# Reordered work at the seams of a two-block transformer kernel: squares with eight buffers, weight halves and loads in another order

## The reference

```python
# block 1
xn = rms_norm(h, norm_mix_g);  proj = xn @ w_in        # q, k, v of stick-breaking attention, q, k, v, g of retention
h = h + (g_sb * (y_sb @ w_sb_out) + g_ret * (y_ret @ w_ret_out)) @ w_out
hn = rms_norm(h, norm_ffn_g)
# 4 groups of 4 experts: best group, its two best experts, each (silu(x @ w_gate) * (x @ w_up)) @ w_down
h = h + hierarchical_moe(hn, ...);  h = rms_norm(h, norm_final_g)
# block 2
proj = rmsnorm(x, norm_mix_g) @ w_in                   # sparse attention with a top-128 index, and q_b, k_b, v_b
x = x + heads @ w_out
x = x + cross_attention(rmsnorm(x, norm_cross_g), rmsnorm(mem, norm_mem_g)) @ w_o_cross     # 256 memory tokens
x = x + square(relu(rmsnorm(x, norm_mlp_g) @ w_up)) @ w_down
return rmsnorm(x, norm_final_g)
```

## Time and profile before

| | |
|---|---|
| median of three runs | 1749.81 us |
| profiled execution | 1747.31 us |
| its span | 1745.5 us |
| PE busy | 1640.7 us (94%) |
| DVE busy | 949.8 us (54%) |
| ACT busy | 747.6 us (43%) |
| POOL busy | 648.5 us (37%) |
| clock of PE granted over the span | 0.978 |

### The profile page before, as it was taken

One profiled execution on the slowest core, in us unless ns is written; L12 is line 12 of the kernel. 1 busy time (PEld: TensorE's weight loads), 2 busy tenths in 40 slices (PEclk: granted clock), 3 DMA queues, 4 the chain that ended last, 5 costly groups with the idle time before them and its releaser, 6 DMA issues. The chain is left out here.

```text
span 1745.5 us, 21103 instructions
## 1 busy us (share of the span) xinstructions
PE 1640.7 (94%) x7992; PEld 1331.5 (76%) x7992; DVE 949.8 (54%) x1123; ACT 747.6 (43%) x895; POOL 648.5 (37%) x261
## 2 busy tenths in 40 slices
PE   7999999899999899999947989899999999999996
PEld 7898788668787888888846857766786788888884
DVE  6514310377164589999857779694443454141413
ACT  6344413234334588888834142475324332222221
POOL 1332154313434133442234726563331434343441
PEclk9999999999999999999978989999999999999998
DMA  6421034212223699999942313400321222222221
GB/s 236 144 73 49 25 110 141 102 35 95 97 101 125 269 422 421 392 387 394 382 166 86 125 49 109 136 1 1 140 77 33 87 97 97 96 96 97 97 96 48
DMA packets 46740, 250.31 MB, mean 143 GB/s; under 512 B 9456, under 2 KB 10224, under 8 KB 19920
## 3 DMA queue, kind: packets, MB, share of 16 engines
q1 hardware_dynamic: 40912, 238.89, 36.9%
q0 software_dynamic: 5184, 8.40, 1.3%
q10 hardware_dynamic: 576, 2.10, 0.3%
HBM read 239.20 MB, written 14.68 MB: 145 GB/s over the span
## 5 line engine op out<-in xcount | busy, mean ns | idle before, releaser
L148 POOL TENSOR_TENSOR w_lo<-raw,w_hi 128x2048 fp32r<-128x2048 f32 x95 | 437.6, 4607 | 704.5 <-ACT w_hi L142 704.4
L227 PE MATMUL psum<-x_hi,w_hi 128*128 128x512 f32 x840 | 329.6, 392 | 10.8 <-POOL w_lo L148 5.9
L228 PE MATMUL psum<-x_lo,w_hi 128*128 128x512 f32 x840 | 327.0, 389 | 0.0
L229 PE MATMUL psum<-x_hi,w_lo 128*128 128x512 f32 x840 | 326.9, 389 | 0.0
L142 ACT ACTIVATE w_hi<-raw 128x2048 fp32r<-128x2048 f32 x100 | 191.0, 1910 | 317.1 <-PE psum L229 315.6
L1296 DVE TENSOR_TENSOR moe_lo<-moe_w,moe_hi 128x2048 fp32r<-128x2048 f32 x99 | 225.6, 2291 | 31.7 <-ACT moe_hi L1286 30.7
L1286 ACT ACTIVATE moe_hi<-moe_w 128x2048 fp32r<-128x2048 f32 x99 | 189.3, 1915 | 27.0 <-PE psum L229 21.4
L227 PEld LDWEIGHTS psum<-x_hi,w_hi 128*128 128x128 f32 x840 | 157.7, 188 | 47.8 <-DVE x_lo L402 5.7
L228 PEld LDWEIGHTS psum<-x_lo,w_hi 128*128 128x128 f32 x840 | 157.7, 188 | 33.1 <-issue 0.7
L229 PEld LDWEIGHTS psum<-x_hi,w_lo 128*128 128x128 f32 x840 | 157.7, 188 | 33.0
L429 DVE TENSOR_TENSOR res<-res,psum 128x512 f32<-128x512 f32 x56 | 38.4, 687 | 217.6 <-PE psum L229 217.6
(11 more groups left out here) (369 smaller groups left out, 2999.8 us busy)
## 6 DMA issues: line engine op xcount, KB each, us to landing
raw<-in_w_dense SPq DMA_DIRECT2D x101, 1024.0 KB, 4.8
moe_w<-in_w_moe_ahead SPq DMA_DIRECT2D x54, 1024.0 KB, 14.2
moe_w<-in_w_moe SPq DMA_DIRECT2D x48, 1024.0 KB, 14.6
yrow<-expert_rows SPq DMA_DIRECT2D x8, 512.0 KB, 10.0
res<-in_x SPq DMA_DIRECT2D x4, 512.0 KB, 11.2
decay<-in_decay SPq DMA_DIRECT2D x8, 256.0 KB, 3.8
hn_rows<-hn_tok ACTq DMA_DIRECT2D x4, 512.0 KB, 2.7
out<-res SPq DMA_DIRECT2D x4, 512.0 KB, 2.6
```

What stands on the lines that cost most here:

```text
L148: pool.tensor_tensor(w_lo[c % RING][:, :], raw[c % RING][:, :], w_hi[c % RING][:, :].bitcast(F32), ALU.subtract).then_inc(lo_ready, 1)
L227: pe.matmul(out, lh, rh, start=first, stop=False)
L228: pe.matmul(out, lh, rl, start=False, stop=False)
L229: return pe.matmul(out, ll, rh, start=False, stop=last)
```

## The change

Six things are edited. (1) `Norm` takes further square buffers (`more_sq`); norm1 has eight, so its squares wait for no add. (2) At start-up SP issues chunk 2 ahead of the third group of x, ACT and DVE take three squares, gained copies and low halves before chunk 2's halves, and PE runs 30 warm-up products in place of 26. (3) In `residual_act` the eighth block's gained copy stands ahead of the next chunk's high half. (4) The memory's high half moves from 96 to 88 KB, off the third expert chunk's high buffer; that chunk is split within k_mem; SP loads expert chunks 0 to 2 at once and 3 to 5 after both gathers have landed; PE reads the number of rounds within k_mem. (5) The low half of q_idx's first chunk goes from POOL to DVE. (6) In q_rope, q_b and k_b POOL makes the low half ahead of the rotation's adds.

```diff
     def dense_pool(pool, name, after=None, halves_first=False):
...
-                if after:
+                if after and not halves_first:
                     after(pool, i, b)
                 split_lo(pool, c0 + 2 + b, i)
+                if after and halves_first:
+                    after(pool, i, b)
...
         def square(self, act, kt):
-            if kt >= 2:
-                act.wait_ge(n_added, (KT - 1) * self.u + kt - 1)
-            act.activation(self.sq[kt % 2][:, :], self.x[:, kt, :], ACT.Square).then_inc(n_squared, 1)
+            if kt >= len(self.sq):
+                act.wait_ge(n_added, (KT - 1) * self.u + max(1, kt - len(self.sq)))
+            act.activation(self.sq[kt % len(self.sq)][:, :], self.x[:, kt, :], ACT.Square).then_inc(n_squared, 1)
...
         for t in range(KT):
-            if t % 2 == 1:
+            if t % 2 == 1 and t < KT - 1:
                 split_hi(act, c0 + 2 + t // 2, t0 + t + 1)
             act.wait_ge(bank_free, t0 + t + 5)
             if gained:
                 gained(t)
+            if t == KT - 1:
+                split_hi(act, c0 + 2 + t // 2, t0 + t + 1)
             norm.square(act, t)
...
-    norm1 = Norm("norm1", res, "mix", 152, hi=x_hi, lo=x_lo, bank=4)
+    norm1 = Norm("norm1", res, "mix", 152, hi=x_hi, lo=x_lo, bank=4, more_sq=(144, 146, 148, 150, 164, 166))
...
         for g in range(4):
+            if g == 2:
+                load_chunk(sp, 2)
             sp.dma_start(res[:, 2 * g:2 * g + 2, :], d["x"][:, 2 * g:2 * g + 2, :]).then_inc(x_landed[g], 16)
-        load_chunk(sp, 2)
...
-        split_lo(dve, 2)
         norm1.add_square(dve, 2)
         x_low(2)
+        split_lo(dve, 2)
...
         square(0)
+        square(1)
         v_mem_out(0)
-        square(1)
         x_high(0)
         x_high(1)
+        square(2)
+        x_high(2)
         v_mem_out(1)
         split_hi(act, 2, 2)
-        square(2)
-        x_high(2)
...
-        for _ in range(26):
+        for _ in range(30):
...
-    m_high = at("mem_hi", 96, [P, KT, MEM], FR)
+    m_high = at("mem_hi", 88, [P, KT, MEM], FR)
...
-            if c == 2:
-                sp.wait_ge(hn_stored, 32)
+            if c == 3:
+                sp.wait_ge(xg_landed[0], 16)
+                sp.wait_ge(xg_landed[1], 16)
             sp.dma_start(ring[c][:, :], d["w_moe_ahead"][PAIRS - 1, c]).then_inc(moe_landed[c // 2], 16)
...
-                             5: lambda: moe_rows_t(pe, 0, 0)})
+                             5: lambda: [moe_rows_t(pe, 0, 0), rounds_read.append(rounds_of(pe))]})
...
             moe_split_chunk(act, 0, 1)
+            moe_split_chunk(act, 0, 2)
...
-        for b in range(2):
-            moe_low_chunk(dve, 0, b)
-            moe_rows_low(dve, 0, b)
+        moe_low_chunk(dve, 0, 0)
+        moe_rows_low(dve, 0, 0)
+        moe_low_chunk(dve, 0, 1)
+        moe_low_chunk(dve, 0, 2)
+        moe_rows_low(dve, 0, 1)
...
     def project_gpsimd(pool):
-        split_lo(pool, KEYS_C + 2)
...
+        pool.wait_ge(lo_ready, KEYS_C + 3)
         split_lo(pool, KEYS_C + 3)
...
-            dense_pool(pool, name, after=lambda e, i, b: rot2.pool(e, name, b))
+            dense_pool(pool, name, after=lambda e, i, b: rot2.pool(e, name, b), halves_first=True)
...
         dve.tensor_tensor(kc_t[0][:, :], psum[:, (KEYS_T + 1) % 4, :], cos_k[:, :], ALU.mult).then_inc(bank_free, 1)
+        dve.wait_ge(lo_ready, KEYS_C + 2)
+        split_lo(dve, KEYS_C + 2)
```

More of the change, by code:

```diff
@@ L176, in dense_sync, with dense_pool @@
         loop(sp, n, body)
-    def dense_pool(pool, name, after=None):
+    def dense_pool(pool, name, after=None, halves_first=False):
         n, k = turns(name)
@@ L287, in __init__ @@
         def __init__(self, tag, x, gain, temps_kb, n_tok=S, hi=None, lo=None, out=None, bank=0,
-                     rstd_kb=None, y_kb=None, sums=True, deferred=False):
+                     rstd_kb=None, y_kb=None, sums=True, deferred=False, more_sq=()):
             self.x, self.gain, self.n, self.hi, self.lo, self.out, self.bank = x, gain, n_tok, hi, lo, out, bank
@@ L296, in __init__ @@
             if sums:
-                self.sq = [at(f"{tag}_sq{b}", temps_kb + w * b, [P, n_tok]) for b in range(2)]
+                self.sq = [at(f"{tag}_sq{b}", kb, [P, n_tok])
+                           for b, kb in enumerate((temps_kb, temps_kb + w) + more_sq)]
                 self.sum = at(f"{tag}_sum", temps_kb + 2 * w, [P, n_tok])
@@ L362, in add_square @@
             if kt == 1:
-                a, b = self.sq
+                a, b = self.sq[:2]
             else:
-                a, b = self.sum, self.sq[kt % 2]
+                a, b = self.sum, self.sq[kt % len(self.sq)]
                 dve.wait_ge(n_added, (KT - 1) * self.u + kt - 1)
@@ L1318, in route_sync @@
         sp.dma_start(kc_rows, kc_out[:, :, :]).then_inc(kv_moved, 16)
+    rounds_read = []
     def route_tensor(pe):
@@ L1523, in rounds_of, with expert_loop @@
         return eng.value_load(rounds_i[0:1, 0:1], min_val=1, max_val=TB)
-    def expert_loop(eng, body):
-        n_rounds = rounds_of(eng)
+    def expert_loop(eng, body, n_rounds=None):
+        n_rounds = rounds_of(eng) if n_rounds is None else n_rounds
         with eng.Fori(0, n_rounds) as r:
@@ L1632, in body @@
             down(n, 1, 1)
-        expert_loop(pe, body)
+        expert_loop(pe, body, rounds_read[0])
     def moe_scalar(act):
@@ L1674, in body @@
             read_down(n, 1, 1)
-        moe_split_chunk(act, 0, 2)
         expert_loop(act, body)
@@ L1708, in body @@
             moe_low_chunk(dve, n + 1, 2)
-        moe_low_chunk(dve, 0, 2)
         expert_loop(dve, body)
```

## The result

The changed kernel takes 1733.7 us (median of 4 runs, 1731.05 to 1735.58) against 1750.49 before (4 runs): ratio 0.9903, 95% interval 0.9886 to 0.992, 16.8 us less. Run again beside other kernels it took 1729.8 us (1729.33 to 1733.92), 20.6 us less than the 1750.44 measured with it, ratio 0.989 [0.9875, 0.9904]. The forecast of 1733.3 was right as a total, and both medians lie in its range of 1729 to 1738. Several of its terms were not right, and their errors cancel.

What follows compares the result with a forecast made beforehand. TensorE was taken to bound the kernel, so only its idle time or granted clock matters. Terms 4.2 + 0.1 + 2.8 + 1.84 + 2.7 + 4.9 = 16.5 us took 1747.31 to 1730.8; plus 2.5 for the median, 1733.3, range 1729 to 1738.

Steps and rivals of the forecast that it cites:

- Start-up (4.2): Start-up to sb_q: PE's idles before chunks 2 and 3 go, the one before chunk 4 shrinks; 4.2 us, bounds 3.0 to 5.3.
- The step on transfers: Start-up loads: with nothing ahead chunk 2 lands at 18.6 us; chunk 3, queued behind more bytes, near 25.4.
- Out seam (+0.1): Seam after layer out: hn's last block goes before the split; at most 0.16 us gained, taken as 0.1.
- Entry (2.8): Entry into expert loop: gather and loop-head idles, 4.5 us, go, but PE waits 2.3 for chunk 6; net 2.8 us.
- q_idx (1.84): Projections after the experts: DVE makes q_idx's first low half in time, so PE's wait goes; 1.84 us, or 1.3.
- rotations (2.7): q_rope, q_b, k_b: low halves ahead of the rotation's adds remove PE's waits of 1.98 and 1.03; 2.7 us.
- seams (4.9): Seams out2 to q_cross and o_cross to up0: x_lo avoids POOL's low half, removing 2.44 us twice; 4.9 us.
- The bank wait: v_b's third tile: PE waits 0.3 us for a bank that DVE frees at 1095.12.
- (a): Rival: transfers give little, start-up gives 1.5 and the entry nothing; 10.9 us saved, 1738.9; chance 0.20.
- (b): Rival: expert loop becomes bound by loads, eight passes lose 20 us; end 3.5 us later, 1753.3; chance 0.03.
- (d): Rival: start-up and seam orders fail, only projections and the gather give; 7.1 us saved, 1742.7; chance 0.04.
- (c): Rival: entry not capped by chunk 6 and start-up gives 5.3; 19.4 us saved, 1730.4; chance 0.09.

Runs made afterwards that it cites:

- the looser wait alone: Kernel before, with a norm's squares waiting only for the add that last reads their buffer, two buffers kept: 1743.77 us, ratio 0.9963.
- the idle filled: Kernel before, with 12 unused products of ones added on TensorE in the idle time ahead of the first query product: 1747.41 us, ratio 0.9986.
- the start-up run: Kernel before with only edits 1 and 2 (square buffers, start-up orders and loads, warm-up products): 1741.32 us, ratio 0.9948.
- the first execution: First profiled execution of the changed kernel: span 1733.8 us, against 1745.5 for the kernel before.
- the second: Second profiled execution of the changed kernel, from its repeat measurement: span 1727.8 us, against 1745.5 for the kernel before.
- the control: The changed kernel itself measured once more, nothing altered, beside three other kernels: 1729.8 us, ratio 0.989 to the kernel before.
- The store edit: Changed kernel, with expert loads waiting for the keys' store only ahead of chunk 10's load, whose place the store reads: 1728.27 us, ratio 0.9874.

## Why the prediction was right, and where it was not

**Start-up (4.2).** 3.5 to 3.7 in the traces, within the bounds; PE's 1.35 us before sb_q met the 1.5 predicted. The step on transfers failed in its use: chunk 2 landed at 19.3 (18.6 said), chunk 3 at 26.3 (25.4 said), late enough to leave 1.00 us. In the two traces with the load order undone sb_q comes 1 us earlier, so all of the gain is that of the squares and ACT's order, 2.46 of it by the looser wait alone. The term also left out the clock. The forecast started from an execution whose clock stayed at 1.00 behind the 3.51 us idle, and added the 2.5 us to the median as a constant; that execution was 2.9 us quicker than the median of the 29 runs. A fall behind this idle, in four traces of five, costs 1.7 to 1.8 us, and the median with the idle filled was 2.4 to 2.8 lower. So the clock there may be about half of the 3.4 us that the start-up run gained beyond its 5.5 us of waits. That is an inference: timed runs carry no clock windows. The four traces with the fall lost 21.0 to 22.4 us of clock from sb_q on while PE was busy, against 20.0 in the one without; and the looser wait alone leaves 2.2 us open with the fall present. The cause of the rest is open.

**Square waits.** The prediction gave them to start-up only. They also act on the memory norm, whose idle of 1.39 us went, and on the last norm (0.65): a term of 2.0 that was not in the sum. The row of the table up to the logits shows 1.10 where 1.1 more of clock was lost, and 2.13 where none was.

**Out seam (+0.1).** Wrong in sign. The prediction looked at hn, which goes ahead of the split, and not at the squares, which stand behind it for the same 1.9 us. ACT's square ended at 549.6 and found POOL's low half begun:

```profile
549.17 4.50 POOL L148 TENSOR_TENSOR w_lo<-raw,w_hi 128x2048 fp32r<-128x2048 f32 x1 [7.59 <-ACT w_hi L142]
```

```profile
549.65 4.58 DVE L370 TENSOR_TENSOR norm_sum<-norm_sum,norm_sq 128x512 f32<-128x512 f32 x1 [2.51 <-ACT norm_sq L343]
```

The last add takes 4.58 us where one without POOL beside it takes 0.68, PE idles 1.49, and the stage loses 1.33 us by it up to the norm's products. In the first execution 3.0 more are lost up to the lists, with 3.4 us more of clock lost than in the kernel before; in the second 0.55, with no more than before. The prediction had told this chain for the seam at q_cross, where the sum had some 2.3 us to spare (1258.7 against 1261), and did not ask it of the seam where PE has not. The Trainium skill, "SBUF — State Buffer", section "Who interferes with whom", has the rule: issue order decides which of two such instructions waits. The trace agrees, and with the square first the idle was gone.

**Entry (2.8).** The term that failed by size. Its steps mostly held: the gather landed in time (no idle at 586.40), the last key eviction ended at 594.5 (595.1 said), PE waited at the fourth projection (2.61, 2.3 said; by the prediction's own times it would have been 1.5, from 613.2 to 614.7), and the store landed at 601.2 (near 600 said), from its issue at 594.57 and the least of these:

```profile
DMA to landing us min/median/max: 6.6/6.7/6.8
```

One did not. The read of the round count was to be all of the 1.87 us at the loop's head; it moved, and 1.68, 1.43 and 1.27 us are still idle in three traces. In all seven traces with the read moved the loop's first product starts 1.19 to 1.22 us behind ACT's last key eviction, for which PE waits just ahead of the loop. That holds even where the eviction ends together with PE's transposes (both at 589.33, product at 590.52, with chunk 2's load back). With the read at the head 1.82 to 1.88 us pass from the last transpose. So the read was about 0.65 us of the 1.87, an estimate from these two; what fills the other 1.2 no run tells. The rest of the idle, up to 0.5 us in the first execution, is the eviction's own delay behind chunk 2's split. The Trainium skill, "Advanced Engine Details and Errata", section "Sequencer and Instruction Queues", lets instructions queue while control runs; no run here shows that as a gain that reaches the end.

PE's idles of 0.25 us and more from the lists to the end of the first pass tell what the entry was worth: 4.76 us in the kernel before (2.63, 1.87, 0.26), 4.58 in the changed kernel without the entry's edits, 4.29 and 4.32 with them, 2.53 with the store's wait moved as well. The forecast had left 2.3. So the edits took 0.3 to 0.5 us of idle away, where the prediction took away 2.5. Chunk 6 took back more than was said (2.6 to 2.9 us in place of 2.3), and the head kept 1.4 to 1.7 us that were put at nothing. With the entry alone the time is the same (1.0001), in the whole the traces give 0.0, and the medians' 3.7 isn't shown to be its own. It was held back by the wait for the store: with that wait moved the trace is 2.4 us better than the control from lists to sums. Besides, the prediction did not ask what else would stand beside the early load of chunk 2: it is the rows' store, which the gather needs.

**q_idx (1.84), rotations (2.7), seams (4.9).** 1.2 to 2.6, 2.7, and 5.1 to 5.7 in the traces; every idle named is gone. The bank wait came as 0.95 us instead of 0.3. Timed alone the projections gave 3.3 to 3.6 of 4.5, and the residual's order 3.6 to 4.2 of 4.9, of which the out seam's 1.3 is the rest.

**The rivals.** (a), slow transfers, is refuted by landings; (b), a loop bound by loads, by PE's waits for moe_h: 2.61 us in the first trace and 2.9 in the second, all before 622 us. (d) held at one point only, the out seam. (c) said 1730.4, and the two medians, 1733.7 and 1729.8, don't tell it from the forecast; the traces do, since the entry was capped by chunk 6 and the start-up gave 3.5 to 3.7 and not 5.3. The store edit took most of that cap away, at 1728.3. Of the signs of being wrong that the prediction named, one was there in part: PE's clock fell behind the out seam in the first execution.

So the waits at start-up, in the projections and at the two seams were forecast rightly, and the total was met by luck: what was left out of the sum, 2.0 us of square waits and the 3.4 us that the start-up gained beyond its waits, stood against the out seam's 1.3 us and an entry that did not come.

## What to carry to other kernels

Ask of every instruction that an order is changed around, not only of the one that moves forward: at a seam the work that feeds the next sum may stand behind the split that was let pass. Where a load is issued early, look for the transfers that it now runs beside, and for what waits for them. A semaphore shared by two loads makes the first as late as the second, and any wait that guards one place of a ring holds all loads behind it: put it at the load that needs it. An idle of a few microseconds on TensorE can cost more than its length, since the clock behind it may fall; take an execution's clock windows before taking it for the median.

## What the runs showed of the hardware

Two executions of one kernel differ by 6.0 us of span and, while PE is busy, by 6.7 us of lost clock. With idles of 2.07 to 3.52 us before sb_q the granted clock was 0.83 to 0.91 over 30 to 50 us in four traces of five; with idles of up to 1.35 us it was 1.00 in all nine. A program with twelve products of which nothing is used in such an idle was 2.4 to 2.8 us faster, by a cause that its trace doesn't show. The last store of the rows, 512 KB, took 2.6 us with no expert load in flight, and 3.8 to 7.4 in six traces in which loads of 1 MB were still under way. PE's first product in a loop came 1.2 us behind the last semaphore that it waited for ahead of the loop, in seven traces of seven.
